# First head of the delta layer in another order, key taps behind the query taps, every fourth weight remainder and the spreading of the substitution on DVE

## The reference

```python
qkv = silu(short_conv_centred(hn @ w_in[:, :3072], conv_w))     # 5 taps a channel
q, k = l2_norm(q), l2_norm(k)
beta = sigmoid(b);  g = -exp(a_log) * softplus(a + dt_bias)     # one per head, direction, token
# per chunk: gc = cumsum(g), decay = exp(gc_i - gc_j)
lower = strict(kb @ k.T * decay);  a_mat = I + lower
u, w  = triangular_solve(a_mat, [v * beta, kb * exp(gc)])
# over the chunks, in order:
v_new = u - w @ state
o     = q_dec @ state + qk @ v_new
state = state * exp(g_last) + k_dec.T @ v_new
# then: rms norm of o per head, * silu(gate), output projection, residual, final rms norm
```

## Time and profile before

| | |
|---|---|
| median of 3 runs | 1423.48 us (1422.72 to 1424.24) |
| the profiled execution: its time, its span | 1425.28 us, 1423.6 us |
| mean granted TensorE clock | 0.987 of full |
| PE busy (matmul) | 1337.1 us, 94% |
| PE weight load, DVE, ACT, POOL busy | 984.1, 803.6, 680.7, 284.4 us |
| the chain that ended last, by engine | PE 70%, DVE 14%, ACT 9%, issue 4%, DMA 2%, POOL 1% |

### The profile page before, as it was taken

The page is one execution under the profiler, slowest core; times in us unless marked ns, Lnnn a source line. Parts: engine busy times, 40 slices in busy tenths (PEclk is TensorE's granted clock), DMA queues, the critical chain, the costliest instruction groups (busy, mean ns, idle before and its releaser), DMA issues.

```text
span 1423.6 us, 25677 instructions
## 1 busy us (share of the span) xinstructions
PE 1337.1 (94%) x9981; PEld 984.1 (69%) x9981; DVE 803.6 (56%) x2210; ACT 680.7 (48%) x1757; POOL 284.4 (20%) x206
## 2 busy tenths in 40 slices
PE   5999999999999998499999999999999999998998
PEld 4866766667544456388777877788778787875543
DVE  6235444444354426867578576675776775852243
ACT  6155464554555425246465463664654736543121
POOL 7211021110011143304122141131220413200000
PEclk9999999999999999799999999999999999999999
DMA  5011010020211111011021110110111101034121
GB/s 184 31 44 31 15 45 16 30 75 30 89 60 60 73 60 47 30 46 31 17 65 41 35 56 17 46 45 32 60 31 46 46 16 61 1 137 175 30 74 74
DMA packets 19416, 74.81 MB, mean 53 GB/s; under 512 B 3040, under 2 KB 3296, under 8 KB 17760
## 3 DMA queue, kind: packets, MB, share of 16 engines
q1 hardware_dynamic: 19296, 73.18, 15.0%
HBM read 61.04 MB, written 12.12 MB: 51 GB/s over the span
## 4 chain that ended last, share of the span: by engine, by line
PE 70%; DVE 14%; ACT 9%; issue 4%; DMA 2%; POOL 1%; SPq 0%; POOLq 0%; DVEq 0%; ACTq 0%
PE bank L1629 16%; PE bank L1726 12%; PE bank L1701 8%; PE bank L1766 4%; PE bank L1656 4%; PE bank L1682 3%; PE bank L1741 3%; PE bank L1667 3%; DVE arena L1531 2%; PE bank L1900 2%; PE bank L1914 2%; PE bank L1825 2%; PE bank L1917 2%; DVE arena L1391 2%; DVE arena L1533 2%
## 5 line engine op out<-in xcount | busy, mean ns | idle before, releaser
L1726 PE MATMUL bank<-hn_hi,w_hi 128*128 128x512 f32 x512 | 225.6, 441 | 17.5 <-ACT arena L1049 17.5
L1726 PE MATMUL bank<-hn_hi,w_lo 128*128 128x512 f32 x512 | 203.8, 398 | 0.0
L1726 PE MATMUL bank<-hn_lo,w_hi 128*128 128x512 f32 x512 | 203.0, 397 | 0.0
L1629 PE MATMUL bank<-hn_hi,w_hi 128*128 128x512 f32 x320 | 136.8, 428 | 0.5 <-ACT arena L984 0.3
L916 POOL TENSOR_TENSOR w_lo<-arena,w_hi 128x1024 fp32r<-128x1024 f32 x30 | 76.7, 2557 | 298.8 <-ACT w_hi L1080 298.8
L1629 PE MATMUL bank<-hn_hi,w_lo 128*128 128x512 f32 x320 | 125.9, 394 | 0.0
L1629 PE MATMUL bank<-hn_lo,w_hi 128*128 128x512 f32 x320 | 125.8, 393 | 0.0
L1726 PEld LDWEIGHTS bank<-hn_hi,w_hi 128*128 128x128 f32 x512 | 98.3, 192 | 36.4 <-ACT arena L1049 20.4
L1701 PE MATMUL bank<-arena 128*128 128x512 f32 x256 | 119.0, 598 | 0.0
L1726 PEld LDWEIGHTS bank<-hn_hi,w_lo 128*128 128x128 f32 x512 | 97.8, 191 | 22.7
L1263 DVE CUSTOM_DVE_ANT_0 arena<-bank,arena 128x384 f32<-128x384 f32 (+1 forms) x128 | 70.1, 582 | 67.0 <-issue 66.7
(11 more groups left out here) (231 smaller groups left out, 2670.8 us busy)
## 6 DMA issues: line engine op xcount, KB each, us to landing
arena<-in_w SPq DMA_DIRECT2D x52, 512.0 KB, 3.6
arena<-in_x SPq DMA_DIRECT2D x16, 512.0 KB, 4.5
arena<-gc_scratch SPq DMA_DIRECT2D x8, 1024.0 KB, 5.0
x_scratch<-arena SPq DMA_DIRECT2D x8, 512.0 KB, 2.6
arena<-x_scratch SPq DMA_DIRECT2D x8, 512.0 KB, 3.7
out<-arena SPq DMA_DIRECT2D x8, 512.0 KB, 2.6
oT_scratch<-arena SPq DMA_DIRECT2D x7, 512.0 KB, 4.9
arena<-oT_scratch SPq DMA_DIRECT2D x7, 512.0 KB, 8.1
```

The costliest lines, as they stand in the source:

```text
L1629: ins = te.matmul(bank[r % 2][:], wp[:, tile % 2, k], hp[:, k, hf * HALF:(hf + 1) * HALF], start=(k == 0 and m == 0), stop=(k == KT - 1 an ...
L1726: ins = te.matmul(b[:], wp[:, t % 2, k], hp[:, k, hf * HALF:(hf + 1) * HALF], start=(k == 0 and m == 0), stop=(k == KT - 1 and m == 2))
```

## The change

It leaves layer 0 and the arithmetic as they are and does five things.

1. In the first head, projections and chain are interleaved in other portions (56 items ahead of the spreading in place of 57; 7 between `gtr` and `gcum`; 5 in place of 14 between the gates and the key transposes). The constants of the inversion are set up in DVE's waits for the gates, except for `level_rows(1)`, which stands between `wqk` and the substitution.
2. In the first head, the four additions to `ET` are done by DVE and no longer by POOL.
3. In `inversion(h)` the five key taps of the next head come straight behind the query taps.
4. The remainder of tiles 8, 12, 16, 20, 24 and 28 is computed by DVE, at a new event `wrest` behind the spreading, in place of POOL at the event `ws`.
5. The spreading (`init`) is done by DVE, in two instructions for one of POOL.

```diff
@@ inversion(h)
                 conv("Q", h, 3, 4)
                 put(("silu", "Q", h))
+                conv("K", nxt, 0, 1, 2, 3, 4)
                 f(2)
                 if h == B_HEADS - 1:
                     put(("finld",))
...
                 stage("x6", h)
-                conv("K", nxt, 0, 1)
...
                     put(("onorm", prev))
-                conv("K", nxt, 2, 3, 4)
@@ the first head
             put(("gl", 1))
-            f(2)
+            f(1)
             put(("gtr",))
-            f(2)
-            put(("gcum",))
-            f(2)
-            put(("gctr",))
-            f(2)
+            f(7)
+            put(("gcum",), ("gctr",))
+            f(1)
             conv("K", 0, 0, 1, 2, 3, 4)
             put(("silu", "K", 0), ("tab1", 0), ("etm", 0, 0), ("etm", 0, 1))
-            f(14)
-            put(("lev",), ("ktr", 0, 0), ("ktr", 0, 1), ("ssq", 0))
-            f(2)
+            f(4)
+            put(("ktr", 0, 0), ("ktr", 0, 1), ("ssq", 0))
+            f(4)
             put(("gramk", 0, 0), ("gramk", 0, 1), ("tabx", 0), ("ete", 0, 0), ("ete", 0, 1), ("stab", 0),
                 *[("wqk", 0, g, cc) for g in range(2) for cc in range(4)])
-            put(("subc", 0, 0), ("subc", 0, 1), ("diag", 0, 0), ("diag", 0, 1))
-            f(4)
-            put(*sub_pieces(0))
-            f(21)
+            f(6)
+            put(("lev",), ("subc", 0, 0), ("subc", 0, 1), ("diag", 0, 0), ("diag", 0, 1), *sub_pieces(0))
+            f(25)
             put(*spread(0))
@@ the heads after
-  22: sub[24:] + spread(h),
+  22: sub[24:] + spread(h) + [("wrest", 4 * h + 4)] * (h < B_HEADS - 1),
@@ POOL
                 if e[0] == "ws":
                     t = e[1]
+                    if by_dve(t):                    # t % 4 == 0 and t >= 8
+                        continue
                     pool.wait_ge(w_rounded, t + 1)
+                    pool.wait_ge(w_split, t)
...
-                elif e[0] == "init":
-                    ...
@@ DVE
+            def level_rows(d):
+                link(ve.tensor_tensor(vpp[:, 6 + d], vpp[:, 4], cum[:, 1 - d], ALU.mult))
+                for rows in quads:
+                    link(ve.scalar_tensor_tensor(lev4[rows, d], vpp[rows, 6 + d, rows], -1.0, ident[rows, rows],
+                                                 ALU.mult, ALU.subtract))
+                    for rnd in range(2):
+                        link(ve.tensor_copy(inE[rows, rnd, d], bc(ident[rows, rows], 4)))
...
+                elif e[0] == "etm" and e[1] == 0:
+                    d = e[2]
+                    dve.wait_ge(consts, 3 + 3 + 4 + 2)
+                    link(ve.tensor_tensor(ET[:, d], ET[:, d], bc(emask[:, d], NT), ALU.add))
+                    dve.wait_ge(tab_dve, 1)
+                    ve.tensor_tensor(ET[:, d], ET[:, d], bc(head_tab2[:, 0, 2, NT * d:NT * d + NT], P, 2), ALU.add).then_inc(et_masked, 1)
...
+                elif e[0] == "wrest":
+                    t = e[1]
+                    dve.wait_ge(w_rounded, t + 1)
+                    dve.wait_ge(w_split, t)
+                    ve.tensor_tensor(w_lo[:, t % 2], ring1[:, t % 2], w_hi[:, t % 2].bitcast(F32), ALU.subtract).then_inc(w_split, 1)
...
+                elif e[0] == "init":
+                    h, rnd, p = e[1:]
+                    d, lo = unit_group(rnd, p)
+                    dve.wait_ge(sub_done, h + 1)
+                    for q in range(2):
+                        ins = ve.tensor_scalar(tri[:, rnd, p, 1, :, 2 * BLK * q:2 * BLK * (q + 1)],
+                                               sub_blk[:, 8 * d + lo:8 * d + lo + 4], q_mask[:, q:q + 1], None, ALU.mult)
+                    ins.then_inc(tt_init[p], 1)
```

More of the change, by code:

```diff
@@ L661, in hybrid_encoder_kernel, with by_dve @@
         EV = layer1_order()
+        def by_dve(t):
+            return t % 4 == 0 and t >= 8
         def gate_of(h):
@@ L914, in _ @@
                     t = e[1]
+                    if by_dve(t):
+                        continue
                     pool.wait_ge(w_rounded, t + 1)
+                    pool.wait_ge(w_split, t)
                     gp.tensor_tensor(w_lo[:, t % 2], ring1[:, t % 2], w_hi[:, t % 2].bitcast(F32), ALU.subtract).then_inc(w_split, 1)
-                elif e[0] == "etm":
+                elif e[0] == "etm" and e[1] > 0:
                     h, d = e[1], e[2]
@@ L921, in _ @@
                     gp.tensor_tensor(ET[:, d], ET[:, d], bc(emask[:, d], NT), ALU.add).then_inc(pch, 1)
[L922 removed]
+                    pool.wait_ge(pch, 6 + 2 * h + d)
                     gp.tensor_tensor(ET[:, d], ET[:, d], bc(head_tab2[:, h % 2, 2, NT * d:NT * d + NT], P, 2), ALU.add).then_inc(et_masked, 1)
@@ L1312, in _ @@
                 ve.tensor_copy(baT[:, hf * HALF:(hf + 1) * HALF], bank[2 + hf][0:32, :]).then_inc(ba_copied, 1)
+                if hf == 0:
+                    dve.wait_ge(consts, 3 + 3 + 4 + 2)
+                    part = vpp[:, 1, 0:1].bitcast(I32)
+                    code, odd, pair = (vpp[:, 5, n:n + 1].bitcast(I32) for n in range(3))
+                    link(ve.tensor_scalar(odd, part, 1, None, ALU.bitwise_and))
+                    link(ve.tensor_scalar(pair, part, 3, None, ALU.logical_shift_right))
+                    link(ve.tensor_scalar(pair, pair, 2, None, ALU.bitwise_and))
+                    link(ve.tensor_tensor(code, odd, pair, ALU.bitwise_or))
+                    for n in range(4):
+                        link(ve.tensor_scalar(dh_mask[:, n:n + 1], code, float(n), None, ALU.is_equal))
+                    link(ve.tensor_scalar(code, part, 5, None, ALU.logical_shift_right))
+                    link(ve.tensor_scalar(code, code, 1, None, ALU.bitwise_and))
+                    for n in range(2):
+                        link(ve.tensor_scalar(q_mask[:, n:n + 1], code, float(n), None, ALU.is_equal))
+                    link(ve.tensor_tensor(vpp[:, 2].bitcast(I32), iv, jv, ALU.bitwise_xor))
+                    link(ve.tensor_scalar(vpp[:, 3].bitcast(I32), vpp[:, 2].bitcast(I32), LV0, None, ALU.logical_shift_right))
+                    link(ve.tensor_scalar(vpp[:, 4], vpp[:, 3].bitcast(I32), 1.0, None, ALU.is_equal))
+                    ve.memset(invT, 0.0)
             dve.wait_ge(ba_act, 1)
@@ L1322, in _ @@
             ve.tensor_scalar(gtmp[:, 2], gtmp[:, 2], 1.0, None, ALU.add).then_inc(ba_dve, 1)
+            level_rows(0)
             dve.wait_ge(ba_act, 4)
@@ L1356, in _ @@
                 if e[0] == "lev":
[L1357 to L1377, removed]
-                    link(ve.memset(invT, 0.0))
+                    level_rows(1)
+                elif e[0] == "etm" and e[1] == 0:
+                    d = e[2]
+                    dve.wait_ge(consts, 3 + 3 + 4 + 2)
+                    link(ve.tensor_tensor(ET[:, d], ET[:, d], bc(emask[:, d], NT), ALU.add))
+                    dve.wait_ge(tab_dve, 1)
+                    ve.tensor_tensor(ET[:, d], ET[:, d], bc(head_tab2[:, 0, 2, NT * d:NT * d + NT], P, 2), ALU.add).then_inc(et_masked, 1)
                 elif e[0] == "conv":
```

10 lines of the change are left out of this document (1 added, 9 removed).

## The result

The changed kernel took 1387.49 us in the median of 4 runs (1384.75 to 1390.66), the kernel before, timed beside it, 1423.86 (1422.72 to 1427.17): a ratio of 0.9742, 95% interval 0.9710 to 0.9774. That is 36.4 us faster.

What follows compares the result with a forecast made beforehand. PE was taken as the bound, busy 94% of the span, a head being its work plus listed waits. -11.3 + 2.6 - 8.5 - 11.1 + 2.6 = -25.7 gave 1397.8 us off the median; range up to 1410, mechanism alone 1391 to 1404.

Steps and rivals of the forecast that it cites:

- First head up to `v0`: First head's chain: earlier gates and constants moved into DVE's waits bring the first `v0` to 589.5, 10.0 us earlier.
- the first rival: First head held elsewhere: low clock after 7 us idle, two splits on the substitution; gives 3 not 11, 1406 us; 12%.
- (b): First head, key transposes to `ET` exponentials: end at 563.8; DVE's four additions, 5.2 us, end near 559.3, hidden.
- Behind the first `v0`: First head: the four `v0`, paced by POOL at 1.55 each, need at most 1.12 on PE; another 1.3 us gained.
- First inversion: Key tile K1 evicted later, split on the taps, `y5` copies queued behind them: PE waits 2.6 us at `x6`.
- Before `v0` in heads 1 to 6: POOL's split and the 1.07 wait go, spreading 0.3 less: 1.38 a head, 8.5 us with head 7.
- Both go: 1.85 x 6 = 11.1: Key taps, heads 1 to 6: PE's waits of 1.43 (eviction) and 0.42 (silu) vanish, 11.1 us; bounds 4 and 13.
- Last head: Last projection item falls behind `x5`, so the final loads start later: 2.6 us lost, bounds 1 and 3.
- The eviction wait: Rival, projections: PE meets ACT's silu and table loads at the next bank, 11.1 us lost, 1409 us; 10%.
- the taps did not collide in heads 1 to 6: Rival, every inversion: taps collide twice and come late, each head pays 2.6 us, 1413 us; 8%.
- no copies were late there: Slower rival: `y5` copies behind the taps on DVE hold `x6`; 1428 us at 5 us a head; 4%.
- refilled by the recurrence: No-change rival: PE's waits shrink but are refilled by the recurrence's waits, 1423 us; 3%.

Runs made afterwards that it cites:

- e_etm: The changed kernel with the four additions to `ET` in the first head back on POOL (part 2 undone): 1386.41 us, ratio 0.9731.
- b_last: The changed kernel with 3 items in place of 2 behind the silu of the queries in the last head, ahead of its `x5`: 1383.56 us, ratio 0.9713.
- b_h0: The changed kernel with the key taps of head 1 alone back at their old places in the first inversion: 1381.83 us, ratio 0.9704.
- a_wrest: The kernel before with part 4 alone, remainders on DVE and the spreading still on POOL: 1424.31 us, ratio 0.9996.
- d_noinit: The changed kernel with the spreading back on POOL (part 5 undone), remainders still on DVE: 1401.43 us, ratio 0.9842.
- a_taps: The kernel before with part 3 alone, the five key taps of the next head behind the query taps: 1402.89 us, ratio 0.9840.
- a_first: The kernel before with parts 1 and 2 alone (first head's order, constants, additions on DVE): 1420.01 us, ratio 0.9968.
- e_lev: The changed kernel with all constants of the inversion in one block ahead of the key transposes: 1393.94 us, ratio 0.9781.

## Why the forecast was wrong in size

**First head up to `v0`: right.** Forecast -10.0, measured -9.16. Each step came within 0.9 us: key transposes 554.7 forecast and 554.23 measured, with 7 us of idle forecast and 6.13 measured; `wqk` 563.9 and 564.28; the substitution 570.8 and 571.22; `v0` 589.5 and 590.30. The 0.50 clock lay over the key transposes (553.5 to 560.0) and two splits over the substitution, as the first rival had it, but they did not spoil the sum, so that rival is refuted here. e_etm confirms that part 2 is hidden, as (b) had it, and that it was hidden on POOL as well.

**Behind the first `v0`.** Forecast -1.3, measured -3.7: from `v0` to `x4` are 6.02 us, where they were 9.72. Of these 3.7 us, 2.1 are the `v0` themselves: 1.3 for POOL's pace, as forecast, and 0.8 because, issued together, they take 0.9 each and not 1.12. The other 1.6 were not forecast, and they are luck: the projections between `v0` and `x4` met the low clock before, and hardly any of it after (the granted clock is the number behind POOL's).

```profile
605.10:609.00 3.90, 3.90 (x13) 2.81 (x9) 0.70 (x2) 1.60 (x3) 0.00 (x0) 0.50 0.00 0
```

```profile
593.90:596.30 2.40, 2.40 (x11) 1.74 (x9) 2.33 (x3) 0.10 (x1) 0.00 (x0) 0.93 0.00 0
```

And 1.5 of the 3.7 is lost at once, because the second round of `x4` waits 1.31 for ACT.

**First inversion.** Forecast +2.6; from `y5` to `y6` it took 12.97 us where it had taken 8.81, +4.16. Of that 2.7 are the late taps (b_last against b_h0), as forecast and by the mechanism that was named (the late key tile, the collision with the split, the copies queued behind), and 1.5 the lowered clock behind the two waits, which the term left out.

**Before `v0` in heads 1 to 6: right, a little small.** The 1.07 vanished, and so did DVE's stall of 2.17 at the end of the substitution (a split now falls on its start, where an instruction takes 2.08 at 658.50). The wait before `v0` fell by 0.18 where 0.3 was written. What I did not see is that part 4 needs part 5: a_wrest and d_noinit show that with POOL still spreading, the remainder blocks it for 0.8 us a head, and the longer wait meets the low clock more often.

**The step that failed: "Both go: 1.85 x 6 = 11.1. The small waits behind them come from ACT's own row of squares and stay."** Alone, part 3 gave 3.53 us in each of these heads (a_taps), 21 in six, above my bound of 13. The mechanism was right, the size was not. Two errors add up:

1. The small waits did not stay: 0.17 and 0.28 vanished too. ACT reached its squares late for the same reason for which it evicted late: moving the taps alone took these waits away too. That makes 2.31 instead of 1.85.
2. The idle time that the list of waits shows is not all that a wait costs, so a head is not "PE's work plus these waits", as I had put it. Two rows of the kernel before, around the wait of 1.43:

```profile
729.90 0.39 PE L1726 MATMUL bank<-hn_hi,w_lo 128*128 128x512 f32 x1
...
732.05 0.40 PE L1726 MATMUL bank<-hn_lo,w_hi 128*128 128x512 f32 x1
```

Between them is the matmul of 731.71. Without a wait these matmuls start 0.23 us apart (729.67 to 729.90). Here 1.81 lie between the start at 729.90 and the next, 1.58 more than 0.23, where 1.43 is listed; and the one after it starts 0.34 later, not 0.23. So the wait cost 0.15 + 0.11 = 0.26 us above its idle time: the overlap with the matmul before and after it is lost. Over a head the same comes out: (3.53 - 2.31) / 4 waits = 0.3 us for each. To see that nothing else is in it, I set a period of a_taps beside that of before, matmul by matmul; both have the same 916 in the same order (heads 2 and 4). They drift apart only at the four waits and the few matmuls around them: in head 2 by 1.69, 0.72, 0.64 and 0.43 us, where 1.42, 0.42, 0.17 and 0.26 are listed. With the whole change the list counts 5.44 us of waits a head before and 1.95 after, 3.49 less, and the period is 5.36 less (88.0 instead of 93.36): 3.53 by part 3, and 1.83 by parts 4 and 5, where 1.38 was forecast. I had summed idle times, which is a lower bound, and set my upper bound from the same column.

**Last head: right, then the clock.** +2.6 forecast, 2.7 by the comparison with d_noinit. The other 2.7 of the +5.38 is the lowered clock: 178.44 - 173.86 = 4.6 in this execution, less 173.06 - 171.15 = 1.9 in that of before. It fits that the four runs lie in two pairs, near 1384.8 and 1390.4, whose mean granted clocks are 0.991 to 0.992 and 0.988 to 0.989.

**The other rivals.** The eviction wait did not move to the next bank (0.5 us left of 17.5), the taps did not collide in heads 1 to 6 (POOL's split came at 705.82, behind them), and no copies were late there; a_taps shows that even a collision in every head would have fitted into the hole. PE's waits were not refilled by the recurrence: 0.49 a head came where 0.41 went. In a_wrest and d_noinit a DVE pass over two SBUF operands starts 0.2 us ahead of a GpSimd instruction, and the spreading takes 3.15 us where it had taken 2.33. The rule on the shared port (the Trainium skill, SBUF — State Buffer, section Who interferes with whom) agrees with this: the one that comes second is blocked. I had weighed it for the split and not for the spreading, which mattered only where part 4 stood without part 5.

## What to carry to other kernels

On the engine that bounds the kernel, count a wait that you remove at its idle time plus what the pipeline loses around it (0.3 us each here, more than the shortest of these waits itself), and check the sum against the distance between two equal points of the loop, not against the list of waits. Ask of every small wait behind a large one whether it has the same cause, since then it goes too. Two moves that meet on a shared resource have no price of their own: part 4 was worth nothing without part 5, and part 5 was worth 13.9 us in the whole and 5.8 alone. In an order written by hand, one filler item at the head of the queue (25 or 26) can decide where every later one falls.

## What the runs showed of the hardware

The granted clock fell behind much shorter waits than the 9 us of the earlier trace rows. In the kernel before, `v0` follows a wait of about 1.64 us in heads 1 to 7. Two of these heads, which differ (the granted clock is the number behind POOL's):

```profile
784.00:787.00 3.00, 3.00 (x68) 2.72 (x65) 0.00 (x0) 1.54 (x4) 1.45 (x3) 1.00 0.02 5
877.50:880.50 3.00, 3.00 (x61) 2.74 (x57) 0.00 (x0) 1.54 (x4) 1.29 (x3) 0.69 0.00 0
```

The period that starts in the second is 94.74 instead of 93.3: 1.4 us for a stretch at the lower level (1.2 instead of 2.4 GHz). Counted over heads 1 to 6 of all profiled executions:

| Wait before `v0` | Executions | Heads | Heads with low clock at `v0` |
|---|---|---|---|
| 1.64 us | before, a_taps, a_first | 18 | 4 (1, 2, 1) |
| 2.46 us | a_wrest, d_noinit | 12 | 7 (3, 4) |
| 1.47 us and less | the changed kernel and the eight others | 54 | none |

Where a like period stands beside it, such a stretch costs 1.0 to 1.5 us. (a_first has two more, behind waits of 1.99 at the key transposes, which cost 0.1 to 0.2.) It is a matter of the execution too: behind the same two waits at `x6` (1.52 and 0.90 us) the changed kernel, d_noinit and e_lev met the low clock, and b_last and e_etm did not. In the tail, behind waits of 2.6 to 3.6 us, most executions met it and some did not. So a shorter wait saved more than itself in these executions; why one head is hit and its equal is not stays open.
